# The opening of a gated-conv and pooling decoder step: loads held to two in flight per queue, transposes written ahead of matmuls, norms in pairs, and later weights in unused rows

## The chip, the cores and the metric

The kernel runs on the 8 cores of one Trainium2 chip. Each core takes one prompt sequence of 2048 tokens and 128 sampled tokens (16 short sequences of 8), and holds all weights in turn; the cores exchange nothing. The metric is the device time of the slowest core in microseconds. Below, TensorE is PE, VectorE is DVE, ScalarE is ACT, GpSimd is POOL and SyncE is SP.

## The reference

```python
def layer(x, ...):
    h = rmsnorm(x, g_pre_mix)
    p = h @ w_in                      # columns [xv | B | C | u | gate_conv | gate_pool], 1024 each
    z = C * xv
    y = B * (z[t-2]*w0 + z[t-1]*w1 + z[t]*w2)          # causal conv of width 3, per channel
    ya = y @ w_out_conv
    yb = pool_scale * groupwise_linear(trailing_mean(u) - u)   # windows 2, 4, 8, 16
    merged = sigmoid(gate_conv) * ya + sigmoid(gate_pool) * yb
    x = x + rmsnorm(merged @ w_o, g_post_mix)
    f = jnp.square(jax.nn.relu(rmsnorm(x, g_pre_mlp) @ w_up)) @ w_down     # 1024 -> 4096 -> 1024
    return x + rmsnorm(f, g_post_mlp)
```

The model width is 1024, the inner MLP width 4096, the depth 1. The last rows of z and u go out as new state.

## The kernel before

A core's 2176 tokens are 17 **tiles** of 128 tokens, x tile 0 to 16. All work is recorded in program order by a small layer (`Prog`) that derives each wait from overlapping rows of SBUF or PSUM; every engine then runs its own instructions strictly in the order in which they were recorded. Since helpers record the operations, the lines of the profile are those of the helpers: L144 is a matmul, L148 a transpose on PE, L161 an activation, L164 a DVE operation on two tensors, L169 one on a tensor and a scalar, L174 one with a scalar and two tensors, L553 a reciprocal, L129 any DMA.

The conv part comes first. Its weights are 8 column blocks j; for each, three chunks c = 0, 1, 2 (the columns of xv, C and B), each 512 KB in HBM and 256 KB once cast to bf16. One unit (j, tg) is column block j over a group tg of 512 tokens: 3 x 8 matmuls into three PSUM banks, then `a_ew` on ACT and DVE: copy xv (ACT), z = C * xv (DVE), the first conv tap cv0 (ACT), then whatever is in the list `mid`, then the taps cv1 and cv2 and the product Ap with B (all three DVE).

An x tile i becomes usable to PE in these steps: load (SP), `x_stat` (square-sum and square root, both ACT), `x_scale` (reciprocal on DVE, then the normalised tile xn on DVE or, where the call says "act", on ACT), `x_tr` (8 transposes on PE into one bank, then evacT on DVE, which copies it to SBUF). `x_norm` is stat and scale together.

The opening (`head`, `head2`, `head3`) runs units (0, 0), (1, 0), (0, 1) and (2, 0) while the first 8 tiles are still arriving. There, `h_mm(j, tg, c, subs)` issues 8 matmuls of 128 columns for each tile in `subs`; with `None` in place of a list it issues 8 of 512 columns. 22 dummy matmuls (`warm`) run first. From the first 512-column matmul of unit (2, 0) on, all units follow one another at 24 matmuls of 512 columns each.

Loads: SP issues x tiles 0 to 7 without a wait. POOL issues the nine chunks of j = 0, 1, 2 without a wait, then chunk (3, 0), which waits for x tile 7; SP's tile 8 waits for chunk (3, 0). Chunks of j = 4 to 7 go where a planner (`Arena`) puts them. It places every later weight load in SBUF, in 220 trials with varied preferences, and issues each load at the step where its rows have come free; the best plan is the one with the lowest cost for loads that come later than a wanted lead. The loads of the conv chunks have no lead: for these it takes the place that is free earliest and, between equals, the lowest address. All weight loads but those of w_down's products are issued by POOL; these, the x tiles, and the reloads of the first residual (x1) are issued by SP.

The last part, w_down for the second half of the tokens, is a series of steps of 16 matmuls of 512 columns. The second last product's weights are (2, q) and the last one's (6, q), q = 0 to 3, of 512 KB each; the first step that uses the (6, q) needs all four, at its matmuls 1, 5, 9 and 13. Their rows come free late, from products 1 and 7 and from x1 tiles (8 to 11) that a DVE addition has used up.

Of the kernel before, what the change touches and what calls it, by code (L numbers as in the profile page):

```python
# [273 lines left out]
class Arena:  # L274
# [19 lines left out]
    @staticmethod  # L294
    def place(keys, first, last, needs, fixed, trial):
        blocks = [(a // UNIT, -(-(a + n) // UNIT), f, l) for a, n, f, l in fixed]
        off, at, cost, state = {}, {}, 0, trial * 7919 + 17
        top = AR_BYTES // UNIT
        for key in keys:
            need = needs[key]  # L300
            n, early = -(-need["n"] // UNIT), need.get("early", 0)
            f, l, lead = first[key], last[key] + need.get("hold", 0), need.get("lead")
            state = (state * 1103515245 + 12345) % (1 << 31)
            how = (state >> 16) % 4 if trial else 0
            best = None
            starts = sorted({0} | {b[1] for b in blocks} | {b[0] - n for b in blocks})
            for c in starts:
                if c < 0 or c + n > top:
                    continue
                free = early  # L310
                for lo, hi, bf, bl in blocks:
                    if lo < c + n and hi > c:
                        if bl < f:
                            free = max(free, bl + 1)
                        elif bf <= l:
                            free = None
                            break
                if free is None or free > f:
                    continue
                late = max(0, free - f + lead) if lead is not None else free  # L320
                cand = (late,) + ((-free, c), (c, 0), (-c, 0), (-free, -c))[how if lead is not None else 1]
                if best is None or cand < best[0]:
                    best = (cand, c, free)
            if best is None:
                return None
            _, c, free = best
            if lead is not None:
                cost += (100 * max(0, free - f + lead) // max(lead, 1)) ** 2 * need.get("cost", 1)
                free = max(free, f - lead)
            off[key] = c * UNIT  # L330
            at.setdefault(free, []).append((f, key))
            blocks.append((c, c + n, free, l))
        return cost, off, at


def build_program():
# [34 lines left out]
    def xsrc(i):  # L371
        return x_p[i * 128:(i + 1) * 128, :] if i < 16 else x_s[:, :]
# [5 lines left out]
    with stack:  # L378
# [49 lines left out]
        def bank():  # L428
            b = min((i for i in range(8) if i not in held), key=lambda i: bank_used[i])
            touch(b)  # L430
            return b
# [28 lines left out]
        def step(w, fn):  # L460
            steps.append({"w": w, "f": fn})
# [45 lines left out]
        xload = {}  # L507

        def load_x(i, deps=()):
            xload[i] = P.dma("sp", XS[i % 11], xsrc(i), "x%d" % (i % 11), name="xload", deps=deps)  # L510
# [22 lines left out]
        def to_hT(src, i, gcol):  # L533

            b = bank()
            pb = PS[:, b, :].bitcast(BF16)
            for k in range(KC):
                P.tr(pb[:, k * 128:(k + 1) * 128], src[:, k * 128:(k + 1) * 128], IDB[:, :], signal=(k == KC - 1))
            gb = bass.AP(CS, gcol, [[72, 128], [1, KC], [0, 128]])
            P.tt("dve", htile(i), pb.rearrange("p (k t) -> p k t", t=128), gb, ALU.mult,  # L540
                 name="evacT")
            touch(b)
# [3 lines left out]
        def x_stat(i):  # L546
            ss = x_ss[i] = stat()
            P.act(XN[i % 3], XS[i % 11], AF.Square, accum_out=ss, name="sq")
            P.act(ss, ss, AF.Sqrt, bias=cs(C_EPS), scale=1.0 / D, name="sqrt")

        def x_scale(i, eng="dve"):
            ss = x_ss[i]
            P.add("dve", lambda e: e.reciprocal(ss, ss), reads=[ss], writes=[ss], name="rstd")  # L553
            if eng == "act":
                P.act(XN[i % 3], XS[i % 11], AF.Identity, scale=ss, name="xn")
            else:
                P.ts(eng, XN[i % 3], XS[i % 11], ss, None, ALU.mult, name="xn")

        def x_norm(i, eng="dve"):
            x_stat(i)  # L560
            x_scale(i, eng)

        def x_tr(i):
            to_hT(XN[i % 3], i, C_GM)
# [10 lines left out]
        def a_keys(h, j):  # L575
            return [("a", h, j, c) for c in range(3)] if h == 0 else [("a", h, j)]

        def a_mm(j, tg, banks, cols=None, cset=(0, 1, 2)):
            h = 0 if tg < 2 else 1
            c0, n, kind = TGS[tg]  # L580
            lo, hi = cols or (0, n)
            for c in cset:
                wt = chunk(("a", 0, j, c), 0) if h == 0 else chunk(("a", h, j), c)
                for k in range(KC):
                    P.mm(PS[:, banks[c], lo:hi], wt[:, k, :], hx(k, c0 + lo, hi - lo), start=(k == 0), stop=(k == KC - 1))
# [58 lines left out]
        def h_mm(j, tg, c, subs):  # L644
            bk = hb.setdefault((j, tg), [])
            while len(bk) <= c:
                bk.append(bank())
                held.add(bk[-1])
            if subs is None:
                a_mm(j, tg, bk, None, (c,))  # L650
            else:
                for s_ in subs:
                    a_mm(j, tg, bk, (s_ * 128, s_ * 128 + 128), (c,))

        def h_ew(j, tg, mid=()):
            held.difference_update(hb[j, tg])
            a_ew(j, tg, hb.pop((j, tg)), mid)

        def head():
            for z in Z + [ZX]:  # L660
                P.memset("dve", z[:, 0:2], 0.0)
            warm(22)
            x_norm(0)
            x_norm(1)
            x_tr(0)
            h_mm(0, 0, 0, (0,))
            x_tr(1)
            h_mm(0, 0, 1, (0,))
            x_norm(2, "act")
            h_mm(0, 0, 0, (1,))  # L670
            h_mm(0, 0, 1, (1,))
            h_mm(0, 0, 2, (0, 1))
            x_tr(2)
            x_norm(3)
            for c in range(3):
                h_mm(0, 0, c, (2,))
            x_tr(3)
            h_mm(1, 0, 0, (0, 1, 2))
            x_norm(4, "act")
            for c in range(3):  # L680
                h_mm(0, 0, c, (3,))
            x_tr(4)
            h_mm(1, 0, 0, (3,))
            h_mm(1, 0, 1, (0, 1, 2, 3))
            x_norm(5)
            h_ew(0, 0, [lambda: x_tr(5)])
        step(a_keys(0, 0) + a_keys(0, 1), head)

        def head2():
            h_mm(1, 0, 2, (0, 1, 2, 3))  # L690
            x_norm(6, "act")
            h_ew(1, 0, [lambda: x_tr(6)])
            for s_ in range(2):
                for c in range(3):
                    h_mm(0, 1, c, (s_,))
            x_norm(7)
        step(a_keys(0, 0) + a_keys(0, 1), head2)

        def head3():
            for c in range(3):  # L700
                h_mm(0, 1, c, (2,))
            x_tr(7)
            h_mm(2, 0, 0, None)
            for c in range(3):
                h_mm(0, 1, c, (3,))
            h_ew(0, 1)
            h_mm(2, 0, 1, None)
            h_mm(2, 0, 2, None)
            h_ew(2, 0)
# [620 lines left out]
        wl = {}  # L1330
# [5 lines left out]
        def issue(key, deps=()):  # L1336
# [13 lines left out]
            dst = arv(off, BF16, list(src.shape[1:])) if len(src.shape) == 3 else arv(off, BF16, [n])  # L1350
            wl[key] = P.dma("pool", dst, src, "w%d" % off, name="wload", deps=deps)

        for i in range(8):
            load_x(i)
        for s, st in enumerate(steps):
            for _, key in W.at.get(s, ()):
                deps = ()
                if key == ("a", 0, 3, 0):
                    deps = [xload[7]]
                issue(key, deps)  # L1360
                if key == ("a", 0, 3, 2):
                    for i in range(8, 11):
                        load_x(i, [wl[("a", 0, 3, 0)]] if i == 8 else ())
                if key == ("a", 0, 7, 2):
                    P.dma("pool", WPG[:, :, :, :], w_pg, "wpg")
            for first, i0 in ((n_u0 + 17, 0), (n_u1 + 18, 12)):
                if first <= s < first + 4:
                    load_xl(i0 + s - first, "xa%d" % (s - first))
            st["f"]()
            if s in u_steps:  # L1370
                unit(u_steps[s])
# [56 lines left out]
```

How the kernel before makes its waits and increments, by code:

```python
    def emit(self, stack):  # L185
# [33 lines left out]
                            continue  # L219
                        key = d.eng
                        val = d.wait_val
                        assert val is not None, (d.name, op.name)
                    if waited.get(key, 0) >= val:
                        continue
                    if need.get(key, 0) < val:
                        need[key] = val
                for key, val in need.items():
                    waited[key] = val
                    eng.wait_ge(sems[key], val)
                    nwait += 1
                if op.fn is not None:
                    ins = op.fn(eng)
                    if op.dma is not None:
                        ins.then_inc(sems[("dma", op.dma[0])], 16)
                    elif op.signal:
                        ins.then_inc(sems[e], 1)
        return nwait
```

## Time and profile before

| What | us |
|---|---|
| median of 3 runs (960.63 to 1078.2) | 961.12 |
| the profiled execution, its own time | 960.17 |
| its span on the slowest core, core 5 | 959.1 |
| busy time of PE, core 5 | 938.4 |
| busy time of DVE, core 5 | 640.3 |
| busy time of ACT, core 5 | 354.2 |

The span runs from the first to the last instruction of one core; the time of an execution is that of the slowest core and 1.07 us more. The profile is one execution. The spans of the other seven cores in it are 954.3 to 958.4 us. The highest of the three runs lies in a disturbed state of the chip and is compared with nothing.

### The profile page before, as it was taken

How to read it: one execution, taken by the hardware profiler on the slowest of the kernel's cores; microseconds unless marked ns; L12 is line 12 of the kernel's file. 1: busy time of each engine (PE TensorE's matmuls, PEld its weight loads, DVE VectorE, ACT ScalarE, POOL GpSimd, SP SyncE). 2: the span in 40 equal slices, each digit the busy share in tenths (PEclk: the TensorE clock that was granted, in tenths of full speed). 3: DMA queues.
4: the chain of work that ended last, by engine and by line, in shares of the span. 5: the costliest groups of instructions: out<-in, count | busy, mean ns of one | idle time of the engine just before them, and what ended most of it. 6: DMA issues, size and time to landing. Idle time of an engine off the chain costs nothing.

```text
span 959.1 us, 15642 instructions; the slowest of 8 cores (954.3 to 959.1 us)
## 1 busy us (share of the span) xinstructions
PE 938.4 (98%) x5158; PEld 463.5 (48%) x5158; DVE 640.3 (67%) x1017; ACT 354.2 (37%) x707; POOL 51.4 (5%) x99
## 2 busy tenths in 40 slices
PE   6899999999999999999999999999999999999997
PEld 4744544444455455455544444444444545544443
DVE  2568886885677777678735655670778887662687
ACT  4344332222433444333334444422023656731032
POOL 2031000000000000000000000000000000000000
PEclk7799999999999999999999999999999999999999
DMA  9999689859889998755227775375692973363683
GB/s 226 256 186 196 132 178 178 165 132 155 152 180 201 192 201 184 119 147 122 78 44 165 169 182 112 86 247 153 163 259 86 165 134 102 102 198 101 188 286 150
DMA packets 70687, 155.13 MB, mean 162 GB/s; under 512 B 22480, under 2 KB 41168, under 8 KB 68304
## 3 DMA queue, kind: packets, MB, share of 16 engines
q0 software_dynamic: 13104, 57.15, 36.1%
q1 hardware_dynamic: 56064, 92.49, 32.7%
q10 hardware_dynamic: 1440, 4.49, 1.2%
q8 instruction: 43, 0.70, 0.3%
q14 instruction: 36, 0.29, 0.1%
HBM read 173.11 MB, written 33.69 MB: 216 GB/s over the span
## 4 chain that ended last, share of the span: by engine, by line
PE 91%; DVE 3%; DMA 2%; issue 2%; ACT 1%; POOL 0%; DVEq 0%; ACTq 0%; POOLq 0%; SPq 0%
PE PS L144 90%; DVE AR L164 2%; DMA AR<-w_a 2%; DVE AR L174 1%; PE PS L148 1%; DMA AR<-wd_d 1%; ACT AR L161 1%; POOL AR L129 0%; ACT WPG L161 0%; DVEq L229 0%; DVE STAT L1002 0%; DVE AR L169 0%; ACT STAT L161 0%; DVE STAT L553 0%; POOL AR L514 0%
## 5 line engine op out<-in xcount | busy, mean ns | idle before, releaser
L144 PE MATMUL PS<-AR 128*128 128x512 bf16 (+1 forms) x4920 | 915.7, 348 | 8.0 <-DMA AR<-w_a 5.1
L144 PEld LDWEIGHTS PS<-AR 128*128 128x128 bf16 x4920 | 444.8, 99 | 468.7 <-issue 12.8
L164 DVE TENSOR_TENSOR AR<-AR 128x512 bf16<-128x512 f32 (+13 forms) x353 | 263.7, 778 | 52.2 <-ACT AR L161 34.2
L164 DVE TENSOR_TENSOR AR<-PS,AR 128x512 f32<-128x512 f32 (+1 forms) x235 | 145.3, 642 | 128.8 <-PE PS L144 96.0
L161 ACT ACTIVATE AR<-PS 128x512 f32<-128x512 f32 (+2 forms) x217 | 126.7, 606 | 237.8 <-PE PS L144 205.7
L161 ACT ACTIVATE AR<-AR 128x1024 bf16<-128x1024 f32 (+4 forms) x123 | 93.5, 766 | 145.9 <-DVE AR L164 122.7
L161 ACT ACTIVATE AR<-PS,CS 128x512 f32<-128x512 f32 (+1 forms) x80 | 48.9, 621 | 76.8 <-PE PS L144 64.0
L174 DVE SCALAR_TENSOR_TENSOR AR<-AR,CS 128x512 f32<-128x512 f32 (+1 forms) x80 | 53.7, 671 | 29.8 <-ACT AR L161 13.2
L161 ACT ACTIVATE AR<-AR,CS 128x512 f32<-128x512 f32 (+1 forms) x40 | 26.3, 658 | 98.0 <-DVE AR L164 80.2
L174 DVE SCALAR_TENSOR_TENSOR AR<-AR,STAT 128x1024 bf16<-128x1024 f32 (+2 forms) x35 | 43.8, 1254 | 4.2 <-DVE STAT L451 1.4
L174 DVE SCALAR_TENSOR_TENSOR AR<-AR 128x512 bf16<-128x512 f32 (+4 forms) x52 | 30.5, 587 | 5.6
L451 DVE RECIPROCAL STAT<-STAT 128x1 f32<-128x1 f32 x34 | 5.4, 159 | 42.7 <-ACT STAT L161 42.7
L164 DVE TENSOR_TENSOR AR<-PS,CS 128x1024 bf16<-128x1024 bf16 x17 | 20.7, 1219 | 17.1 <-PE PS L148 17.0
L164 DVE TENSOR_TENSOR AR<-WPG 128x512 bf16<-128x512 f32 (+1 forms) x27 | 16.7, 629 | 20.2 <-ACT WPG L161 20.2
L129 POOL DMA_DIRECT2D AR<-w_up x16 | 8.4, 528 | 341.1 <-PE PS L144 206.2
L174 DVE SCALAR_TENSOR_TENSOR AR<-PS,CS,AR 128x512 f32<-128x512 f32 (+1 forms) x40 | 26.5, 662 | 0.0
L161 ACT ACTIVATE WPG<-PS 128x512 f32<-128x512 f32 x34 | 19.9, 586 | 15.0 <-PE PS L144 13.0
L129 POOL DMA_DIRECT2D AR<-w_a x32 | 17.1, 559 | 130.5 <-PE PS L144 99.6
L174 DVE SCALAR_TENSOR_TENSOR AR<-PS,STAT,AR 128x1024 f32<-128x1024 f32 x17 | 21.8, 1283 | 2.4 <-DVE STAT L451 1.6
L161 ACT ACTIVATE STAT<-STAT,CS 128x1 f32<-128x1 f32 x67 | 19.7, 294 | 6.0
L144 PE MATMUL PS<-AR,WPG 128*128 128x512 bf16 (+1 forms) x80 | 21.2, 347 | 0.0
L148 PE MATMUL PS<-IDB,AR 128*128 128x128 bf16 x136 | 12.0, 240 | 3.6 <-ACT AR L161 3.3
(45 smaller groups left out, 130.7 us busy)
## 6 DMA issues: line engine op xcount, KB each, us to landing
AR<-wd_d SPq DMA_DIRECT2D x56, 512.0 KB, 5.7
AR<-x_p SPq DMA_DIRECT2D x32, 512.0 KB, 7.9
AR<-w_up POOLq DMA_DIRECT2D x16, 1024.0 KB, 11.2
wd_d<-AR SPq DMA_DIRECT2D x16, 896.0 KB, 8.7
AR<-w_m POOLq DMA_DIRECT2D x16, 768.0 KB, 9.6
x_d<-AR SPq DMA_DIRECT2D x17, 512.0 KB, 4.3
AR<-x_d SPq DMA_DIRECT2D x17, 512.0 KB, 9.6
AR<-w_dn POOLq DMA_DIRECT2D x16, 512.0 KB, 10.3
```

Of the source, the lines that this page charges most:

```text
L129: op = self.add(q, lambda e: e.dma_start(out=out, in_=in_, **kw), reads=[in_], writes=[out], name=name, dma=(semkey, cnt))
L144: return self.add("pe", lambda e: e.matmul(out, lhsT, rhs, start=start, stop=stop, skip_group_check=skip), reads=[lhsT, rhs], writes=[out] ...
L148: return self.add("pe", lambda e: e.transpose(out, in_, ident), reads=[in_, ident], writes=[out], signal=signal, name="tr")
L161: return self.add("act", lambda e: e.activation(out, in_, func, **kw), reads=rd, writes=wr, name=name)
L164: return self.add(eng, lambda e: e.tensor_tensor(out, in0, in1, op), reads=[in0, in1], writes=[out], name=name)
L174: return self.add(eng, lambda e: e.scalar_tensor_tensor(out, in0, scalar, in1, op0, op1), reads=rd, writes=[out], name=name)
L451: P.add("dve", lambda e: e.reciprocal(ss, ss), reads=[ss], writes=[ss], name="rstd")
```

## The change

`head` and `head2` are written in another order: both transposes of tiles 0 and 1 stand before the first matmuls, matmuls go tile by tile and not chunk by chunk, the norms are called in pairs, and the norms of tiles 6 and 7 are in the `mid` lists of units (0, 0) and (1, 0), where transposes of tiles 5 and 6 stood. x tiles 2 to 7 wait for the tile two before, chunks 2 to 8 for the chunk two before. The planner now prefers, for loads without a lead and between places that are free equally early, rows that no earlier load has used.

```diff
@@ Arena.place @@
-                free = early
+                free = 0
...
-                if free is None or free > f:
+                if free is None or max(free, early) > f:
                     continue
+                used, free = free, max(free, early)
                 late = max(0, free - f + lead) if lead is not None else free
-                cand = (late,) + ((-free, c), (c, 0), (-c, 0), (-free, -c))[how if lead is not None else 1]
+                cand = (late,) + ((-free, c), (c, 0), (-c, 0), (-free, -c), (used, c))[how if lead is not None else 4]
@@ head, head2, head3 @@
             x_norm(0)
             x_norm(1)
             x_tr(0)
-            h_mm(0, 0, 0, (0,))
             x_tr(1)
-            h_mm(0, 0, 1, (0,))
-            x_norm(2, "act")
-            h_mm(0, 0, 0, (1,))
-            h_mm(0, 0, 1, (1,))
-            h_mm(0, 0, 2, (0, 1))
+            for s_ in range(2):
+                for c in range(3):
+                    h_mm(0, 0, c, (s_,))
+            x_norm(2)
+            x_norm(3)
             x_tr(2)
-            x_norm(3)
+            h_mm(1, 0, 0, (0, 1))
+            x_tr(3)
             for c in range(3):
                 h_mm(0, 0, c, (2,))
-            x_tr(3)
-            h_mm(1, 0, 0, (0, 1, 2))
-            x_norm(4, "act")
+            h_mm(1, 0, 0, (2,))
+            x_norm(4)
+            x_norm(5, "act")
             for c in range(3):
                 h_mm(0, 0, c, (3,))
             x_tr(4)
             h_mm(1, 0, 0, (3,))
             h_mm(1, 0, 1, (0, 1, 2, 3))
-            x_norm(5)
-            h_ew(0, 0, [lambda: x_tr(5)])
+            x_tr(5)
+            h_ew(0, 0, [lambda: x_norm(6)])
...
             h_mm(1, 0, 2, (0, 1, 2, 3))
-            x_norm(6, "act")
-            h_ew(1, 0, [lambda: x_tr(6)])
+            x_tr(6)
+            h_ew(1, 0, [lambda: x_norm(7)])
             for s_ in range(2):
                 for c in range(3):
                     h_mm(0, 1, c, (s_,))
-            x_norm(7)
+            x_tr(7)
...
             for c in range(3):
                 h_mm(0, 1, c, (2,))
-            x_tr(7)
             h_mm(2, 0, 0, None)
@@ the loads @@
+        chunks = []
         for i in range(8):
-            load_x(i)
+            load_x(i, [xload[i - 2]] if i > 1 else ())
...
-                if key == ("a", 0, 3, 0):
+                if key[:2] == ("a", 0) and key[2] < 3:
+                    chunks.append(key)
+                    if len(chunks) > 2:
+                        deps = [wl[chunks[-3]]]
+                elif key == ("a", 0, 3, 0):
                     deps = [xload[7]]
```

PE in the opening before, from the warm-up to the first 512-column matmuls (`PS<-IDB` is the warm-up, L148 the transposes of one tile):

```order
L144 MATMUL PS<-IDB 128x512 x22
L148 MATMUL PS<-IDB,AR 128x128 x8
L144 MATMUL PS<-AR 128x128 x8
L148 MATMUL PS<-IDB,AR 128x128 x8
L144 MATMUL PS<-AR 128x128 x40
L148 MATMUL PS<-IDB,AR 128x128 x8
L144 MATMUL PS<-AR 128x128 x24
L148 MATMUL PS<-IDB,AR 128x128 x8
L144 MATMUL PS<-AR 128x128 x48
L148 MATMUL PS<-IDB,AR 128x128 x8
L144 MATMUL PS<-AR 128x128 x40
L148 MATMUL PS<-IDB,AR 128x128 x8
```

The same stretch of PE now:

```order
L144 MATMUL PS<-IDB 128x512 x22
L148 MATMUL PS<-IDB,AR 128x128 x16
L144 MATMUL PS<-AR 128x128 x48
L148 MATMUL PS<-IDB,AR 128x128 x8
L144 MATMUL PS<-AR 128x128 x16
L148 MATMUL PS<-IDB,AR 128x128 x8
L144 MATMUL PS<-AR 128x128 x56
L148 MATMUL PS<-IDB,AR 128x128 x8
L144 MATMUL PS<-AR 128x128 x40
L148 MATMUL PS<-IDB,AR 128x128 x8
L144 MATMUL PS<-AR 128x128 x32
L148 MATMUL PS<-IDB,AR 128x128 x8
```

The last line of the first list is tile 5, and the last of the second tile 6. The 48 matmuls behind tiles 0 and 1 are one block whose third group of 8 reads chunk 2; before, 32 of them stood ahead of chunk 2's first use.

DVE from the norm of tile 5 to the second product Ap before (the line with `128x8x128` is an evacT, `PS,AR 128x512` is z or Ap, L174 is cv1 and cv2):

```order
L553 RECIPROCAL STAT<-STAT 128x1
L169 TENSOR_SCALAR AR<-AR,STAT 128x1024
L164 TENSOR_TENSOR AR<-PS,AR 128x512
L164 TENSOR_TENSOR AR<-PS,CS 128x8x128
L174 SCALAR_TENSOR_TENSOR AR<-AR,CS 128x512 x2
L164 TENSOR_TENSOR AR<-PS,AR 128x512
L553 RECIPROCAL STAT<-STAT 128x1
L164 TENSOR_TENSOR AR<-PS,AR 128x512
L164 TENSOR_TENSOR AR<-PS,CS 128x8x128
L174 SCALAR_TENSOR_TENSOR AR<-AR,CS 128x512 x2
L164 TENSOR_TENSOR AR<-PS,AR 128x512
```

DVE now, from the evacuations of tiles 4 and 5 to the same product:

```order
L164 TENSOR_TENSOR AR<-PS,CS 128x8x128 x2
L164 TENSOR_TENSOR AR<-PS,AR 128x512
L554 RECIPROCAL STAT<-STAT 128x1
L169 TENSOR_SCALAR AR<-AR,STAT 128x1024
L174 SCALAR_TENSOR_TENSOR AR<-AR,CS 128x512 x2
L164 TENSOR_TENSOR AR<-PS,AR 128x512
L164 TENSOR_TENSOR AR<-PS,CS 128x8x128
L164 TENSOR_TENSOR AR<-PS,AR 128x512
L554 RECIPROCAL STAT<-STAT 128x1
L169 TENSOR_SCALAR AR<-AR,STAT 128x1024
L174 SCALAR_TENSOR_TENSOR AR<-AR,CS 128x512 x2
L164 TENSOR_TENSOR AR<-PS,AR 128x512
```

The evacT of tile 5 stood behind z of unit (0, 0) and now stands before it; the reciprocal and xn of tile 6, and later of tile 7, now stand between z and cv1. The ACT instructions of these two norms likewise stand behind cv0 of their unit.

SP's last loads before (`wd_d` 128x2048 is one (p, q) weight load, `x_d` a reload of x1):

```order
L129 DMA AR<-x_d 128x1024 x3
L129 DMA AR<-wd_d 128x2048 x4
L129 DMA AR<-x_d 128x1024
L129 DMA AR<-wd_d 128x2048 x3
L129 DMA AR<-x_d 128x4x256
L129 DMA AR<-wd_d 128x2048
L129 DMA AR<-x_d 128x4x256
L129 DMA AR<-x_d 128x1024
```

SP's last loads now:

```order
L129 DMA AR<-x_d 128x1024 x3
L129 DMA AR<-wd_d 128x2048 x4
L129 DMA AR<-x_d 128x1024
L129 DMA AR<-wd_d 128x2048 x2
L129 DMA AR<-x_d 128x4x256
L129 DMA AR<-wd_d 128x2048
L129 DMA AR<-x_d 128x4x256
L129 DMA AR<-wd_d 128x2048
L129 DMA AR<-x_d 128x1024
```

The planner's new plan moves one load each: (6, 1) from behind (6, 0) to the place that (6, 2) had, which waits for the addition of tile 8; (6, 2) to the place of (6, 3), which waits for the addition of tile 9; and (6, 3) behind one more x1 load, where it waits for the last step of product 7 on PE.

## Rows read from the trace of the kernel before

**Rows 1.** Spans of two of the cores, us, and their mean granted clock

```profile
core 1: 958.4 us, clock 0.994
...
core 5: 959.1 us, clock 0.987
```

**Rows 2.** Timeline of PE, opening, core 5: start us, us, instruction, idle before

```profile
15.41 2.72 PE L144 MATMUL PS<-AR 128*128 128x128 bf16 x24 [1.18 <-DMA AR<-w_a]
...
18.97 1.87 PE L144 MATMUL PS<-AR 128*128 128x128 bf16 x16 [0.83 <-DMA AR<-w_a]
...
23.17 2.72 PE L144 MATMUL PS<-AR 128*128 128x128 bf16 x24 [1.48 <-DVE STAT L553]
...
32.68 0.61 PE L148 MATMUL PS<-IDB,AR 128*128 128x128 bf16 x8 [0.29 <-DVE AR L169]
33.13 1.95 PE L144 MATMUL PS<-AR 128*128 128x128 bf16 x32
38.38 1.01 PE L148 MATMUL PS<-IDB,AR 128*128 128x128 bf16 x8 [3.31 <-ACT AR L161]
39.19 6.53 PE L144 MATMUL PS<-AR 128*128 128x128 bf16 x72
...
46.00 1.24 PE L144 MATMUL PS<-AR 128*128 128x512 bf16 x5
```

**Rows 3.** Busy time by stretch, core 5; last columns: PE's granted clock, DMA share, GB/s

```profile
18.90:27.00 8.10, 6.55 (x61) 6.35 (x62) 2.20 (x4) 0.74 (x3) 0.65 (x2) 0.50 1.04 225
27.00:37.30 10.30, 7.79 (x134) 7.39 (x132) 7.18 (x11) 5.23 (x10) 0.95 (x2) 1.00 1.03 190
37.30:44.10 6.80, 5.71 (x55) 5.75 (x56) 4.82 (x7) 3.48 (x6) 0.00 (x0) 0.50 1.04 354
```

**Rows 4.** Timeline of PE, core 1: tile 7 transposed, and the wait near the end

```profile
43.16 0.61 PE L148 MATMUL PS<-IDB,AR 128*128 128x128 bf16 x8
...
929.84 4.48 PE L144 MATMUL PS<-AR 128*128 128x512 bf16 x20 [2.46 <-DMA AR<-wd_d]
```

**Rows 5.** Issues of single weight chunks: 2.0 to 2.3 us, then 48.9 to 49.2 us

```profile
AR<-w_a POOLq DMA_DIRECT2D x1, 256.0 KB, 10.7
...
AR<-w_a POOLq DMA_DIRECT2D x1, 256.0 KB, 4.8
```

**Rows 6.** Timeline of all engines, 31 to 37 us, core 5

```profile
31.41 0.15 DVE L553 RECIPROCAL STAT<-STAT 128x1 f32<-128x1 f32 x1
31.67 0.75 DVE L169 TENSOR_SCALAR AR<-AR,STAT 128x1024 bf16<-128x1024 f32 x1
32.34 0.68 DVE L164 TENSOR_TENSOR AR<-PS,AR 128x512 f32<-128x512 f32 x1
...
33.12 0.72 ACT L161 ACTIVATE AR<-AR,CS 128x512 f32<-128x512 f32 x1 [1.83 <-DVE AR L164]
...
33.40 1.22 DVE L164 TENSOR_TENSOR AR<-PS,CS 128x1024 bf16<-128x1024 bf16 x1 [0.37 <-PE PS L148]
33.75 1.04 ACT L161 ACTIVATE AR<-AR 128x1024 bf16<-128x1024 f32 x1
34.54 1.60 DVE L174 SCALAR_TENSOR_TENSOR AR<-AR,CS 128x512 f32<-128x512 f32 x2
...
34.98 0.30 ACT L161 ACTIVATE STAT<-STAT,CS 128x1 f32<-128x1 f32 x1
36.24 0.69 DVE L164 TENSOR_TENSOR AR<-PS,AR 128x512 bf16<-128x512 f32 x1
```

**Rows 7.** Issue of one weight load of product 6, 922.0 to 922.4 us, core 5

```profile
AR<-wd_d SPq DMA_DIRECT2D x1, 512.0 KB, 8.2
```

**Rows 8.** Timeline, 921 to 931 us, core 5: SP's queue and PE

```profile
922.03 0.33 SPq L129 DMA_DIRECT2D AR<-wd_d  x1
922.82 5.95 SPq L129 DMA_DIRECT2D AR<-x_d  x4
...
930.52 0.81 PE L144 MATMUL PS<-AR 128*128 128x512 bf16 x3 [0.77 <-DMA AR<-wd_d]
```

## The prediction

> **What bounds the kernel now.** I read the spans of the cores first, then PE's timeline through the opening, then the granted clock there, and last the places late in the run where PE waits for a load. PE is busy for 938.4 of core 5's 959.1 us [rows 1], so only the some 20 us in which it isn't, and the stretches in which it runs at half its clock, can be won or lost by a change that removes no work. I call three moments of the opening A, B and C. A is the first use of weight chunk 2, at 18.97 us, which the landing of that chunk set; B is the end of the transposes of tile 5, at 32.68 + 0.61 = 33.29; C is the first 512-column matmul, at 46.00 [rows 2]. Behind C PE has no wait of a microsecond until the last products, so a microsecond at C is one at the end. The reader should see in these rows three kinds of loss before C: waits for chunks (0.83 before A), waits in the ring PE, DVE, ACT (1.48 at 23.17, 3.31 at 38.38), and a low clock: 24 matmuls take 2.72 us at 23.17, and the granted clock is 0.50 (the 1.2 GHz level) from 18.9 to 27.0 and from 37.3 to 44.1, and 1.00 (2.4 GHz) between [rows 3]. At the high level 8 instructions take 33.13 - 32.68 = 0.45 us, 0.056 each; at the low one 2.72 / 24 = 0.113 [rows 2]. The slowest core, 5, is so by its clock and its C: core 1 reaches C at 43.16 + 0.45 = 43.6 and still has a span of 958.4, since it loses 2.46 near the end [rows 1, 4].
>
> **Two in flight.** Of x tiles and chunks, each waits for the second before it. DMA share is 1.04 and 1.03 from 18.9 to 37.3 [rows 3]: the 16 engines are the limit while both queues have work, and two loads in each keep them at work as long as the third is issued and reaches the engines before the second is done. A chunk issued into an empty queue lands after 4.8 us, the first of all after 10.7 [rows 5]. Chunk 2 will be issued when chunk 0 has landed, at about 2.0 + 10.7 = 12.7. Its landing is then between 12.7 + 4.8 = 17.5 and, if it is only drawn on when chunk 1 has landed (at 15.4 by PE's wait for it [rows 2]) and pays 4.8 from there, 20.2. I take A as before, 18.97, since the engines are as full as before; the ends are -1.4 and +1.3. Queued behind the waits are, on SP, only the other x tiles, and on POOL the later chunks and then the chunks of j = 3 to 7; chunk (3, 0) waits for tile 7 as before. Tiles 8 and up and the blocks from j = 3 on are needed behind C, by over 15 us, so I cost their lateness at nothing; that cover is gone only if tile 8 is 15 us late. The Trainium skill (DMA: Bandwidth & Descriptors, section "Anatomy of one DMA — SWDGE (gpsimd) path") speaks against such waits: each DMA issued by GpSimd has a fixed cost of about 2.0 us, which a wait for its completion brings into the open, plus its bytes over 436e3 per us. By it chunk 2 would land 2.0 + 0.6 = 2.6 us behind chunk 0, at 15.3, and the time be some 3.6 us lower than mine; the rows (4.8 in an empty queue) don't agree, and I go by them.
>
> **From A to B.** Before, A to B is 14.3 us. Now 176 instructions stand there in one run: 32 matmuls, tile 2, 16, tile 3, 56, tile 4, 40, tile 5. That is 16 matmuls more than before, since tile 1's matmuls on chunks 0 and 1 now stand behind chunk 2's wait; the idle 1.48 behind tile 2 is filled by 16 matmuls of unit (1, 0). At the high clock 176 take 9.9, at the low one 19.9. Before, on core 5, the clock rose at 27.0, 3.9 us after the unbroken stretch that began at 23.17 [rows 2, 3]; now such a stretch begins at A. So I take 3.9 us at the low level (34 instructions), 142 x 0.056 = 8.0 at the high one, and 0.6 for the wait of tile 2's matmuls on its evacT (1.22 [rows 6], less the 24 instructions ahead of it, and pauses of the issue): 12.5, B = 31.5. The ends are 29.0 and 39.
>
> **From B to C.** This is the term that grows. Before, z of unit (0, 0) stood ahead of tile 5's evacT on DVE, and the norm of tile 6 was done on ACT meanwhile; PE then waited 3.31 for xn of tile 6 and was late with 72 matmuls at the low clock [rows 2]. Now evacT of tile 5 comes ahead of z, and the squares of tile 6 stand behind cv0 on ACT, which waits for z; xn of tile 6 stands ahead of cv1 on DVE, and the same again for unit (1, 0) and tile 7. From the starts in [rows 6], behind B: 0.11 to evacT, 1.14 to z, 0.78 to cv0, 2.16 from cv0's start to the end of the root (33.12 to 35.28), 0.1 to the reciprocal, 0.26 to xn (31.41 to 31.67): 4.55. Then 0.67 to cv1 (as xn to z), 1.70 to Ap (34.54 to 36.24), 0.69 to evacT of tile 6, 1.14 to z of unit (1, 0): 8.75. Then again 0.78, 2.16, 0.1 and 0.26 to xn of tile 7: 12.05, and 0.75 and 0.25 until PE transposes tile 7: 13.05. PE's own work up to there, 32 + 48 matmuls and tile 6, is done before that even at the low clock. Behind it come 0.45 for the transposes and 24 matmuls of unit (0, 1) which before stood ahead of tile 7: 1.4 at the high clock, 2.7 at the low one. C = B + 14.9 to B + 16.2; PE is idle twice for over 1.5 us on the way, as it was before its low clock at 37.3, so I take 15.4: C = 46.9. On core 5 that is 0.9 later than 46.00; on core 1, which had no clock loss ahead of tile 6, 3.3 later than 43.6 [rows 4].
>
> **The planner.** The chunks of j = 4 to 7 go to unused rows, and POOL's issue of 12 chunks no longer waits for PE. PE waited for none of them, so that gains nothing. But the other loads are planned anew, and most of the last ones come a step later. Load (6, 3) was issued at 922.03, landed 8.2 us later [rows 7] and let PE wait 0.77 before the last 4 matmuls of its step [rows 8]. 20 matmuls of 512 columns take 4.48 there, 0.22 each [rows 4]. That step began at 930.52 - 0.77 - 12 x 0.22 = 927.1, and the step before, of 16, at 923.6. Now (6, 2) is issued at 922.03 instead and lands at 930.3; PE needs it 8 matmuls into the step, at 928.9, and waits 1.4. (6, 3) is issued only when PE has ended product 7, at 923.6, behind the x1 load at 922.82. With 8.2 again it lands at 931.8, and later if it queues; I take 933. PE comes to it at 930.3 + 0.9 = 931.2 and waits 1.8. The sum is 3.2 for 0.77: +2.4 on core 5. On core 1, where the same load cost 2.46 [rows 4], I take +3.0. The ends are 0 (a later issue that meets less traffic) and +6.
>
> **Sum.** Core 5: 959.1 + 0.9 + 2.4 = 962.4. Core 1: 958.4 + 3.3 + 3.0 = 964.7, now the slowest [rows 1]. An execution takes 1.07 more than its slowest span (960.17 for 959.1): 965.8. The profiled execution lay 0.95 under the median of the runs; I add little for that: **966**.
>
> **Rivals.** First, *the first chunks come sooner* (faster). With two x tiles queued in place of eight, chunk 0 may not need 10.7 us; at the 4.8 of an empty queue it lands at 6.8 and chunk 2 by 13, and x tiles set the pace: tile 5, which has kept its place, lets B come at about 27.5, C at 43, 4 us below my sum on every core: 962, and with the end unmoved 958. It decides once chunk 2 lands before 16. Against it: x tiles and chunks already shared engines that were full. The Trainium skill (the same page, section "Queues, rings and completion order") says that each DMA engine takes packets in turn from the queues that have work; by that rule the depth of a queue doesn't change the shares, which speaks against this rival too, though no row of mine separates queues. Second, *the parts cancel*: the clock rises by chunk 1's matmuls, or DVE's chain overlaps more than I think, and the loads at the end find less traffic: 961. Third, *the clock stays low*: PE idles from chunk to chunk ahead of A, and if the 1.2 GHz level held up to B, B would be at 38.9 and C at 54, 7 us over my sum: 973.
>
> **How the numbers follow.** My forecast (963 to 971) gets 0.57, the cancelling parts (959 to 963) 0.2, sooner chunks 0.13, the low clock 0.1. The range 958 to 971 leaves out the low clock and half of the sooner chunks, 0.16. Two per cent, about what a measurement of this kernel can tell from no change, are 19 us, from 942 to 980. No case reaches either; for what I haven't seen I leave 0.015 on each side.
>
> **What would show it.** In the changed profile A should stand within 1.5 of 19.0 with PE waiting for `w_a`; a stretch without gaps from A to B with the low clock only at its start; then PE idle ahead of the transposes of tiles 6 and 7, both ended by DVE's xn, and C near 47. Near 930 there should be one or two waits for `wd_d` with 2 to 6 us in all. I am wrong if C is before 44 on core 1, if chunk 2 lands before 16, or if PE doesn't wait for tile 7.

## The result, and the profile after

The changed kernel takes 968.74 us (median of 4 runs, 968.05 to 969.38) against 960.63 for the kernel before (959.62 to 961.12), measured beside it: a ratio of 1.0086, 95% interval 1.0066 to 1.0106. It is slower by some 8 us. As everywhere below, disturbed runs are left out of the medians and the ratio. The forecast was 966, with a range of 958 to 971.

The spans of three cores of the profiled execution, which answer to [rows 1]:

```profile
core 1: 964.0 us, clock 0.989
core 2: 967.0 us, clock 0.987
...
core 5: 966.1 us, clock 0.990
```

Core 1 ends 5.6 us later than before and core 5 7.0; core 2, which took 954.3 before, is now the slowest. To see where the time went I cut each core's span in two, at the end of tile 8's transposes (the first tile behind the opening). Means over the eight cores, from the timeline of PE on each:

| | before | changed | difference |
|---|---|---|---|
| transposes of tile 5 end (B) | 31.7 | 28.7 | -3.0 |
| transposes of tile 8 end | 71.2 | 72.4 | +1.2 |
| from there to the last matmul | 878.2 | 884.0 | +5.8 |
| PE's waits over 0.1 us between 900 and 945 us, sum | 0.6 | 5.1 | +4.5 |

So most of the loss lies near the end of the run, and the opening gains first and then gives back more.

PE in the opening, core 5, to be held against [rows 2] (start us, us, instruction, idle before it and what ended that):

```profile
16.91 3.04 PE L144 MATMUL PS<-AR 128*128 128x128 bf16 x32 [3.13 <-DMA AR<-w_a]
...
28.08 0.61 PE L148 MATMUL PS<-IDB,AR 128*128 128x128 bf16 x8
28.53 1.95 PE L144 MATMUL PS<-AR 128*128 128x128 bf16 x32
35.09 1.01 PE L148 MATMUL PS<-IDB,AR 128*128 128x128 bf16 x8 [4.62 <-DVE AR L169]
35.90 3.85 PE L144 MATMUL PS<-AR 128*128 128x128 bf16 x48
42.50 0.61 PE L148 MATMUL PS<-IDB,AR 128*128 128x128 bf16 x8 [2.75 <-DVE AR L169]
```

A, the use of chunk 2, is at 16.91 in place of 18.97. From there to tile 5 PE has no wait. Then it waits 4.62 us for xn of tile 6 and 2.75 for xn of tile 7, both times for DVE.

Issues of chunk 0 (at 2.0 us) and of chunk 2 (at 10.8 us), core 5, with the time to landing, against the 10.7 of [rows 5]:

```profile
AR<-w_a POOLq DMA_DIRECT2D x1, 256.0 KB, 8.3
...
AR<-w_a POOLq DMA_DIRECT2D x1, 256.0 KB, 5.9
```

Chunk 0 lands 2.4 us sooner. Chunk 2, issued when chunk 0 has landed, takes 5.9 us and is there at 16.8, some 2 us sooner than the chunk that was issued without a wait.

Whose packets the 16 engines move meanwhile, from 8 to 10 us on core 5, before and then in the changed kernel (q0 is POOL's queue, with the chunks, q1 SP's, with the x tiles; packets, MB, share of the engines' time):

```profile
q0 software_dynamic: 87, 0.18, 56.4%
q1 hardware_dynamic: 90, 0.31, 48.8%
```

```profile
q0 software_dynamic: 175, 0.33, 106.5%
q1 hardware_dynamic: 4, 0.00, 0.6%
```

The engines are as full as before, but with other packets. Before, both queues have work and move about as many packets each. Now x tile 2 is issued only at 6.88, when tile 0 has landed, and its packets move from 10 us on. Until then SP's queue is empty, and the chunks have the engines to themselves. It is the same on every core: in these 2 us the chunks move 138 to 175 packets and the x tiles 4 to 11, where before the chunks moved 62 to 87 and the x tiles 66 to 90.

The chain behind tile 5, core 5, ACT and then DVE, against [rows 6]:

```profile
30.77 0.72 ACT L161 ACTIVATE AR<-AR,CS 128x512 f32<-128x512 f32 x1 [4.44 <-DVE AR L164]
31.40 1.04 ACT L161 ACTIVATE AR<-AR 128x1024 bf16<-128x1024 f32 x1
...
32.93 0.29 ACT L161 ACTIVATE STAT<-STAT,CS 128x1 f32<-128x1 f32 x1 [0.40 <-ACT AR L161]
```

```profile
29.94 0.68 DVE L164 TENSOR_TENSOR AR<-PS,AR 128x512 f32<-128x512 f32 x1
33.33 0.16 DVE L554 RECIPROCAL STAT<-STAT 128x1 f32<-128x1 f32 x1 [2.71 <-ACT STAT L161]
34.08 0.87 DVE L169 TENSOR_SCALAR AR<-AR,STAT 128x1024 bf16<-128x1024 f32 x1 [0.59 <-DVE STAT L554]
34.87 1.59 DVE L174 SCALAR_TENSOR_TENSOR AR<-AR,CS 128x512 f32<-128x512 f32 x2
```

These rows are one chain: z (29.94), cv0 (30.77), the squares of tile 6 (31.40), the root (32.93), the reciprocal (33.33), xn (34.08), and only then cv1 (34.87). DVE is idle 2.71 us of it and ACT was idle 4.44 ahead of it.

Busy time by stretch, core 5, of the changed kernel (columns as in [rows 3]): ahead of B, and near the end.

```profile
17.50:20.90 3.40, 3.40 (x36) 3.40 (x34) 0.25 (x1) 0.60 (x1) 0.90 (x2) 0.50 0.98 302
20.90:34.60 13.70, 9.56 (x168) 9.25 (x165) 7.07 (x10) 6.37 (x13) 5.80 (x11) 1.00 0.93 182
```

```profile
928.90:939.10 10.20, 5.25 (x13) 1.62 (x14) 0.76 (x2) 0.64 (x1) 0.00 (x0) 0.50 0.86 294
```

The granted clock rises 4.0 us behind A. Near the end it falls to 0.50, with PE idle for 7.3 of the 9.2 us from 926.5 to 935.7. The 13 matmuls of that stretch take 0.40 us each, against the 0.22 of [rows 4]. Before, the clock was granted in full there (core 5):

```profile
925.00:945.00 20.00, 19.23 (x91) 8.56 (x89) 15.83 (x22) 4.47 (x10) 0.00 (x0) 1.00 0.75 250
```

SP's queue and PE near the end, core 5, against [rows 8], and the issues of the loads (6, 2) and (6, 3) at 919.6 and 921.1 us, against the 8.2 of [rows 7]:

```profile
919.64 0.32 SPq L129 DMA_DIRECT2D AR<-wd_d  x1
920.37 0.52 SPq L129 DMA_DIRECT2D AR<-x_d  x1
921.05 0.57 SPq L129 DMA_DIRECT2D AR<-wd_d  x1
921.74 2.95 SPq L129 DMA_DIRECT2D AR<-x_d  x3
```

```profile
929.35 1.86 PE L144 MATMUL PS<-AR 128*128 128x512 bf16 x4 [2.84 <-DMA AR<-wd_d]
935.71 9.60 PE L144 MATMUL PS<-AR 128*128 128x512 bf16 x36 [4.50 <-DMA AR<-wd_d]
```

```profile
AR<-wd_d SPq DMA_DIRECT2D x1, 512.0 KB, 9.5
...
AR<-wd_d SPq DMA_DIRECT2D x1, 512.0 KB, 14.4
```

The two loads that come a step later than before let PE wait 2.84 and 4.50 us, where there was one wait of 0.77. The second of them takes 14.4 us from issue to landing. It stands behind another load, among four x1 loads and the stores of the results; which of these makes it so long was not tried.

### The profile page after: what moved, and what is told of

It reads as the page before. It is cut to its first block, busy times and chain, and to the rows that moved or that the text cites. A ratio compares the mean times of both kernels' runs of the same rounds, so it can differ in the third digit from the quotient of the medians.

```text
span 967.0 us, 15551 instructions; the slowest of 8 cores (959.3 to 967.0 us)
## 1 busy us (share of the span) xinstructions
PE 935.0 (97%) x5066; PEld 463.3 (48%) x5158; DVE 641.8 (66%) x1019; ACT 351.7 (36%) x705; POOL 51.6 (5%) x99
## 4 chain that ended last, share of the span: by engine, by line
PE 90%; DVE 4%; DMA 3%; issue 2%; ACT 1%; DVEq 0%; SPq 0%; POOL 0%; ACTq 0%; POOLq 0%
PE PS L144 90%; DVE AR L164 2%; DMA AR<-w_a 1%; DMA AR<-wd_d 1%; DVE AR L174 1%; PE PS L148 1%; ACT AR L161 1%; DVE AR L169 0%; ACT STAT L161 0%; DVEq L229 0%; SPq L129 0%; DVE STAT L1002 0%; DVE STAT L554 0%; POOL AR L515 0%; ACTq L229 0%
## 5 line engine op out<-in xcount | busy, mean ns | idle before, releaser
L161 ACT ACTIVATE AR<-PS,CS 128x512 f32<-128x512 f32 (+1 forms) x80 | 48.9, 621 | 77.2 <-PE PS L144 67.7
L174 DVE SCALAR_TENSOR_TENSOR AR<-AR,CS 128x512 f32<-128x512 f32 (+1 forms) x80 | 53.7, 671 | 29.5 <-ACT AR L161 13.4
L174 DVE SCALAR_TENSOR_TENSOR AR<-AR,STAT 128x1024 bf16<-128x1024 f32 (+2 forms) x35 | 43.8, 1254 | 4.1 <-DVE STAT L452 1.0
L174 DVE SCALAR_TENSOR_TENSOR AR<-AR 128x512 bf16<-128x512 f32 (+4 forms) x52 | 30.5, 586 | 6.0 <-DVE AR L164 0.6
L164 DVE TENSOR_TENSOR AR<-WPG 128x512 bf16<-128x512 f32 (+1 forms) x27 | 16.8, 629 | 19.7 <-ACT WPG L161 19.6
L174 DVE SCALAR_TENSOR_TENSOR AR<-PS,CS,AR 128x512 f32<-128x512 f32 (+1 forms) x40 | 26.5, 662 | 0.0
L174 DVE SCALAR_TENSOR_TENSOR AR<-PS,STAT,AR 128x1024 f32<-128x1024 f32 x17 | 21.8, 1284 | 3.0 <-DVE STAT L452 2.5
L148 PE MATMUL PS<-IDB,AR 128*128 128x128 bf16 x136 | 11.3, 231 | 9.1 <-DVE AR L169 9.1
## 6 DMA issues: line engine op xcount, KB each, us to landing
AR<-w_m POOLq DMA_DIRECT2D x16, 768.0 KB, 10.2
```

Of the source, the lines that this page charges most:

```text
L148: return self.add("pe", lambda e: e.transpose(out, in_, ident), reads=[in_, ident], writes=[out], signal=signal, name="tr")
L161: return self.add("act", lambda e: e.activation(out, in_, func, **kw), reads=rd, writes=wr, name=name)
L164: return self.add(eng, lambda e: e.tensor_tensor(out, in0, in1, op), reads=[in0, in1], writes=[out], name=name)
L174: return self.add(eng, lambda e: e.scalar_tensor_tensor(out, in0, scalar, in1, op0, op1), reads=rd, writes=[out], name=name)
```

## The experiments

The theory after the result: three parts act apart. The planner's new plan costs 6 to 8 us near the end; the limit of two in flight gains in the opening; the new order loses there, between B and C. The rival theories: the late waits are a product of the new opening, which shifts the traffic; or the limit only delays loads, and the tiles 6 and 7 are late by it. All kernels compute the whole layer. The table has each run's median, its ratio to the kernel before measured beside it, and means over the cores from the traces: landing of chunks 0 and 2, end of the transposes of tiles 5 and 8, and from there to the last matmul. No run differs from the kernel before by 2%; faster or slower below means that the interval of the ratio leaves out 1. The means are from one profile each. Three kernels are written alike up to tile 8 (changed, old plan, last loads dear) and have it at 72.4, 73.5 and 73.3, so a difference of a microsecond in one column shows nothing by itself.

| run | median | ratio (interval) | chunk 0 | chunk 2 | tile 5 | tile 8 | rest |
|---|---|---|---|---|---|---|---|
| before | | | 12.4 | 18.9 | 31.7 | 71.2 | 878.2 |
| changed | 968.74 | 1.0086 (1.0066 to 1.0106) | 9.7 | 16.5 | 28.7 | 72.4 | 884.0 |
| changed, old plan | 960.89 | 1.0011 (1.0000 to 1.0021) | 9.7 | 16.4 | 29.4 | 73.5 | 877.8 |
| plan only | 967.79 | 1.0080 (1.0063 to 1.0098) | 12.7 | 19.2 | 32.3 | 72.0 | 885.3 |
| limit only | 957.00 | 0.9971 (0.9961 to 0.9981) | 9.9 | 16.6 | 28.6 | 68.2 | 878.2 |
| order only | 962.87 | 1.0031 (1.0019 to 1.0044) | 12.6 | 19.1 | 31.4 | 75.2 | 877.7 |
| limit on x alone | 960.34 | 1.0000 (0.9989 to 1.0010) | 9.7 | 15.8 | 31.7 | 71.0 | 879.1 |
| limit on chunks alone | 963.84 | 1.0040 (1.0024 to 1.0056) | 12.6 | 22.0 | 36.2 | 75.8 | 878.2 |
| three in flight | 959.42 | 0.9989 (0.9978 to 1.0000) | 11.9 | 18.7 | 31.4 | 70.9 | 878.2 |
| changed, last loads dear | 961.17 | 1.0013 (1.0003 to 1.0023) | 10.0 | 16.5 | 29.1 | 73.3 | 877.8 |
| old plan, norms ahead | 956.98 | 0.9967 (0.9951 to 0.9983) | 9.9 | 16.7 | 28.9 | 68.8 | 877.7 |
| both norms ahead | 956.6 | 0.9963 (0.9949 to 0.9977) | 9.8 | 16.5 | 28.7 | 68.4 | 877.8 |

**The changed kernel with the old plan.** The new preference is taken back.

```diff
-                cand = (late,) + (..., (used, c))[how if lead is not None else 4]
+                cand = (late,) + (..., (used, c))[how if lead is not None else 1]
```

> The changed kernel with the planner's preference as it was before. Theory 1 (the loss is the planner's: late weight loads of w_down come a step later): the stretch from the transposes of tile 8 to the last matmul returns from a mean of 884.0 us over the cores to 878.2, the opening stays as in the changed kernel (tile 8 transposed at a mean of 72.4), and the time is 961 to 962, about that of the kernel before. Theory 2 (the late waits come from the new opening, which shifts the traffic of x1 loads and stores against PE): the stretch stays near 884 and the time at 967 to 969.

960.89: theory 1. PE's waits between 900 and 945 us are back at a mean of 0.7 us. On core 5 PE runs through the place without a wait:

```profile
914.76 30.59 PE L144 MATMUL PS<-AR 128*128 128x512 bf16 x141
```

**The plan alone.** The function `place` of the changed kernel, everything else as before.

> The kernel before with the planner's new preference alone. Theory 1 (the planner): the stretch from the transposes of tile 8 to the last matmul grows from a mean of 878.2 us to 883 to 885, the opening stays (tile 8 transposed at 71.2), time 966 to 969. Theory 2 (the new opening is needed for the late waits): the stretch stays near 878, time 960 to 962.

967.79: the plan alone, on the old opening, makes nearly all of the loss. The two waits are there, core 5:

```profile
928.87 1.02 PE L144 MATMUL PS<-AR 128*128 128x512 bf16 x4 [1.58 <-DMA AR<-wd_d]
933.30 12.04 PE L144 MATMUL PS<-AR 128*128 128x512 bf16 x46 [3.40 <-DMA AR<-wd_d]
```

**Last loads dear.** The planner takes the plan whose own sum of lateness is lowest, and that sum counts a late load of the last products like any other. This run keeps the new preference and weights eight loads.

```diff
-                    loads[("dn", half, p, q)] = dict(n=4096, lead=10 if p == 4 else 7)
+                    loads[("dn", half, p, q)] = dict(n=4096, lead=10 if p == 4 else 7, cost=4 if half == 1 and p in (2, 6) else 1)
```

> The changed kernel, with the planner's cost of lateness times four for the weights of products 2 and 6 of the second half. Its plan issues the loads (2, q) and (6, q) at the same steps as the kernel before; the conv chunks stay in unused rows, and the other early loads stand as in the changed kernel. Theory 1 (the loss near the end is the late issue of these eight loads): from the transposes of tile 8 to the last matmul 877.5 to 879 us (884.0 in the changed kernel), time 960 to 962. Theory 2 (something else in the new plan costs, as the chunks that no longer wait, or other late loads): 882 or more, time 965 or more.

961.17, and 877.8 for the rest of the run: theory 1. The chunks in unused rows and POOL's issue without a wait are still in this kernel, and cost nothing that can be seen. SP's queue, core 4, has no weight load behind the one at 919.92, and PE runs on (on core 5 a wait of 1.41 is left; the mean is 0.5):

```profile
919.92 0.32 SPq L129 DMA_DIRECT2D AR<-wd_d  x1
920.36 3.91 SPq L129 DMA_DIRECT2D AR<-x_d  x4
```

```profile
914.82 30.38 PE L144 MATMUL PS<-AR 128*128 128x512 bf16 x138
```

So the late issue of the last weights is what costs, not the use of other rows.

**The limit alone, and the order alone.** Each is the kernel before with one part of the change, copied as it stands in the diff.

> The kernel before with at most two x tiles and two chunks in flight alone. Theory 1 (fewer x tiles share the engines with the first chunks): chunk 2 lands at 16 to 17 in place of 18.9, the transposes of tile 5 end 1.5 to 2.5 us sooner (31.7 before), and those of tile 8 by about 1 to 2 sooner than 71.2; time 959 to 960. Theory 2 (what the changed kernel gains ahead of tile 5 comes from its order, and the waits only delay loads): tile 5 stays at 31.5 to 33, time 961 to 963.

> The kernel before with the new order of head, head2 and head3 alone. Theory 1 (order and limit act apart: the order shortens A to B by some 2 us and lengthens B to C by some 3 to 4): chunk 2 lands at 18.9 as before, the transposes of tile 5 end at about 30.5 to 31, those of tile 8 at 73.5 to 75 (71.2 before), time 963 to 965. Theory 2 (the order costs nothing by itself and the limit makes tiles 6 and 7 late): tile 8 at 71 to 72, time 960 to 962.

Both go the way of theory 1, but not by its sizes: the limit brings 3.0 us at tile 8 where 1 to 2 were expected (and 957.0 for 959 to 960), and the order hardly helps ahead of tile 5. First PE's waits for chunk 2 and for tile 6 on core 5 with the order alone, then the waits behind the transposes of tile 2 and ahead of those of tile 6 with the limit alone, which are as long as before (1.48 and 3.31):

```profile
19.30 3.26 PE L144 MATMUL PS<-AR 128*128 128x128 bf16 x32 [2.19 <-DMA AR<-w_a]
...
37.06 1.01 PE L148 MATMUL PS<-IDB,AR 128*128 128x128 bf16 x8 [4.37 <-DVE AR L169]
```

```profile
20.71 1.50 PE L144 MATMUL PS<-AR 128*128 128x128 bf16 x24 [1.48 <-DVE STAT L553]
...
34.73 1.01 PE L148 MATMUL PS<-IDB,AR 128*128 128x128 bf16 x8 [3.31 <-ACT AR L161]
```

The limit alone makes the kernel faster than before, 0.9971: chunk 2 lands 2.3 us sooner, tile 8 comes 3.0 us sooner (71.2 to 68.2), and the rest of the run stays at 878.2. The order alone makes it 4.0 us later (75.2). It hardly shortens the way from chunk 2 to tile 5 (31.4 - 19.1 = 12.3, before 31.7 - 18.9 = 12.8) and lengthens that from tile 5 to tile 8 from 39.5 to 43.8. I expected A to B to gain 2 us by the order. B is sooner in the changed kernel by the limit, through the landing of chunk 2.

**Which limit pays.** One queue limited at a time.

```diff
@@ limit on x alone: chunks as before @@
-            load_x(i)
+            load_x(i, [xload[i - 2]] if i > 1 else ())
@@ limit on chunks alone: x tiles as before @@
+        chunks = []
...
-                if key == ("a", 0, 3, 0):
+                if key[:2] == ("a", 0) and key[2] < 3:
+                    chunks.append(key)
+                    if len(chunks) > 2:
+                        deps = [wl[chunks[-3]]]
+                elif key == ("a", 0, 3, 0):
                     deps = [xload[7]]
```

> The kernel before with the limit on x tiles alone; the nine chunks are issued without a wait. Theory 1 (x tiles 2 and 3 no longer go ahead of the first chunks on the shared engines; the limit on chunks is no help): chunk 0 lands at 9 to 11 as with both limits, chunk 2 at 14 to 15 (16.6 with both limits), tile 8 is transposed at 67 to 69, time 955 to 957. Theory 2 (each queue has its share of the engines whatever its depth): chunk 0 lands at 12.4 and chunk 2 at 18.9 as before, tile 8 at 71 or later, time 960 to 962. Theory 3 (a deep queue of chunks takes the engines from x tiles 4 to 7): chunk 2 early, but tiles 6 and 7 late, tile 8 at 70 or later, time 959 or more.

> The kernel before with the limit on chunks alone; the eight x tiles are issued without a wait. Theory 1 (the limit on x tiles is what pays): chunk 0 lands at 12 to 13 as before, chunk 2 at 19 to 20.5, since it is issued when chunk 0 has landed and then takes some 6 us; tile 8 at 71 to 73, time 960 to 963. Theory 2 (the limit on chunks is what pays, by leaving the engines to the x tiles): tile 8 at 68 to 69.5, time 957 to 958.5.

I had expected the limit on x to pay alone. It brings the chunks sooner, as theory 1 of that run says (chunk 2 at 15.8), but theory 3 decides the time: nine chunks in their queue now make the x tiles late, and tile 5 is where it was before. From 11 to 16 us on core 5 the queues move 211 and 209 packets, and x tile 5 lands at a mean of 27.7 us (before 21.0, with both limits 22.1). The limit on chunks alone is worse than either theory had: chunk 2 at 22.0 and tile 8 at 75.8. On core 5 PE waits for tile 4 with the limit on x alone, and for chunk 2 with that on chunks alone:

```profile
27.61 0.61 PE L148 MATMUL PS<-IDB,AR 128*128 128x128 bf16 x8 [2.74 <-ACT AR L161]
```

```profile
22.70 1.87 PE L144 MATMUL PS<-AR 128*128 128x128 bf16 x16 [3.43 <-DMA AR<-w_a]
```

With the chunks alone limited, chunk 2 (issued at 13.15, when x tiles 0 to 2 have landed) takes 9.4 us beside the five x tiles still on their way:

```profile
AR<-w_a POOLq DMA_DIRECT2D x1, 256.0 KB, 9.4
```

Either limit alone gives 0 or a loss of 4.5 us at tile 8; both together give 3.0. What pays is that neither queue runs ahead of the other.

**Three in flight.** The diff is against the kernel with the limit alone.

```diff
-            load_x(i, [xload[i - 2]] if i > 1 else ())
+            load_x(i, [xload[i - 3]] if i > 2 else ())
...
-                    if len(chunks) > 2:
-                        deps = [wl[chunks[-3]]]
+                    if len(chunks) > 3:
+                        deps = [wl[chunks[-4]]]
```

> The kernel before with at most three x tiles and three chunks in flight in place of two (order and planner as before). Theory 1 (what pays is that neither queue runs ahead of the other): near the run with two, chunk 2 at 15.5 to 17, tile 8 at 68 to 69, time 956.5 to 958. Theory 2 (a third x tile already goes ahead of chunk 0 and takes its time on the engines): chunk 0 lands at 11 to 12.5, chunk 2 at 17 to 18.5, tile 8 at 69.5 to 71, time 958.5 to 960.5.

Theory 2: chunk 0 lands at 11.9, nearly as late as without a limit, and of the 3.0 us at tile 8 0.3 are left. The third x tile, issued at 2.0 us, keeps SP's queue at work beside chunk 0: from 8 to 10 us on core 5 it moves 67 packets to the chunks' 84, where with two in flight there were 4 to 175.

**Norms ahead.** The changed kernel with the old plan, and:

```diff
-            h_ew(0, 0, [lambda: x_norm(6)])
+            x_norm(6)
+            h_ew(0, 0)
...
-            h_ew(1, 0, [lambda: x_norm(7)])
+            x_norm(7)
+            h_ew(1, 0)
```

> The changed kernel with the planner's preference as it was before and with the norms of tiles 6 and 7 written ahead of the elementwise work of units (0, 0) and (1, 0) in place of inside it. Theory 1 (PE's waits of 4.4 and 1.5 to 2.5 us ahead of the transposes of tiles 6 and 7 come from the chain z, cv0, squares, root, reciprocal, xn): the first of them falls below 1.5, B to the transposes of tile 8 shrinks from 44 us by 3 to 5, tile 8 at 68.5 to 70.5, time 956 to 958. Theory 2 (tiles 6 and 7 are late because their loads are limited): the waits stay, tile 8 at 72 to 74, time 960 to 962.

956.98, tile 8 at 68.8 in place of 73.5, with the loads as limited as before: theory 1. PE ahead of tiles 6 and 7, core 5:

```profile
31.81 0.61 PE L148 MATMUL PS<-IDB,AR 128*128 128x128 bf16 x8 [0.69 <-DVE AR L169]
...
37.94 1.01 PE L148 MATMUL PS<-IDB,AR 128*128 128x128 bf16 x8 [2.84 <-DVE AR L169]
```

The wait for tile 6 has gone from 4.62 (4.50 with the old plan) to 0.69. That for tile 7 stays.

**Both norms ahead.** In addition the squares of tile 7 stand ahead of unit (0, 0), and its reciprocal and xn inside:

```diff
             x_norm(6)
-            h_ew(0, 0)
+            x_stat(7)
+            h_ew(0, 0, [lambda: x_scale(7)])
...
-            x_norm(7)
             h_ew(1, 0)
```

> The kernel of the run before with both norms ahead, with the squares and the root of tile 7 also ahead of unit (0, 0)'s elementwise work and its reciprocal and xn inside it, where DVE waits 0.99 us for cv0. Theory 1 (DVE's chain decides B to C to the end): PE's wait of 2.84 us ahead of tile 7 goes, tile 8 is transposed at 66 to 67.5 (68.75 with tile 6's norm alone out of the chain), time 954 to 956. Theory 2 (the squares of tile 7 hold up xv of unit (0, 0) on ACT, since tile 7 lands as late as 28 to 31 us, and the banks of unit (0, 1) come later by as much): PE waits for a bank in place of tile 7, tile 8 at 68.5 to 70, time 957 to 958.

Between the two: tile 7 is transposed 1.6 us sooner (36.7 in place of 38.3, means of the cores), but tile 8 only 0.4. On core 6 PE no longer waits for xn but for DVE's product Ap of unit (0, 0), which frees a bank:

```profile
36.49 0.61 PE L148 MATMUL PS<-IDB,AR 128*128 128x128 bf16 x8 [1.44 <-DVE AR L164]
```

That is theory 2's wait, though smaller than it said. The time of 956.6 can't be told from that of the run before it or of the limit alone; each of the three is faster than both kernels, than the kernel before by 0.3 to 0.4%. The limit and the old order together with the norms ahead was not tried, nor a better place for the last loads on top.

## Why the prediction came out right, step by step

The time (968.74 for 966) and the sign are those of the forecast. Its terms were less good: two were off, in opposite directions.

- **Chunk 2 at 18.97.** This step failed: "I take A as before, 18.97, since the engines are as full as before". A is at 16.91 on core 5, beyond the end of -1.4 that I gave and the 1.5 that I named as a sign. The landing of chunk 0 at 12.7 was held fast, and it moved: with two x tiles in flight it lands 2.4 us sooner. The rival of the sooner chunks had the mechanism, at a smaller size: it asked for chunk 2 before 16, and it is 16.5 in the mean (15.8 and 15.9 on cores 0 and 6). My argument against it was that the engines are full anyway. They are, but SP's queue runs empty between two x tiles, and the chunks get its share (175 packets to 4 from 8 to 10 us, before 87 to 90). The runs with the limit on x alone (chunk 0 at 9.7) and with three in flight (11.9) show the same: how long the other queue has work decides when the first chunk lands. The Trainium skill's rule (DMA: Bandwidth & Descriptors, section "Queues, rings and completion order") that each engine takes packets in turn from the queues with work was weighed in the same place. The traces agree with it while both queues have work, with 87 packets to 90. What failed is my step from it, that "the depth of a queue doesn't change the shares": a queue held to two in flight is without work part of the time.
- **The price of a chunk.** 4.8 us from issue to landing in an empty queue was the bound, 5.9 is measured. The Trainium skill's sum (the same page, section "Anatomy of one DMA — SWDGE (gpsimd) path"), an estimate of 2.6 us by its figures for 256 KB, is less than half of it; the trace decides.
- **A to B, 12.5.** 28.69 - 16.91 = 11.8: right, with the low clock only at its start, as said (3.4 us of it).
- **B to C, 15.4.** From the end of tile 5 to that of tile 7 plus 1.35 us for 24 matmuls at the high clock: 43.1 + 1.35 - 28.7 = 15.8 on core 5. The chain z, cv0, squares, root, reciprocal, xn is the one that I summed from [rows 6], and the run with the norms ahead shows it to be the cause.
- **The opening as a whole.** I had +0.9 on core 5 and +3.3 on core 1. By the transposes of tile 8 it is -1.7 and +1.5, mainly for the sooner chunk 2.
- **The last loads, +2.4 to +3.0.** This is the term that was mis-sized. Its mechanism is shown by three runs; its measure is +5.8 in the mean, +3.9 on core 1 and 887.03 - 878.46 = +8.57 on core 5, beyond my end of +6. Two things were missing. I gave (6, 3) the 8.2 us of the load before and 1 us for the queue; it takes 14.4. And I priced only the waits. On core 5 these are 7.34 - 0.77 = 6.57 of the 8.57. The clock fell to 0.50 at 928.9, 2.4 us into the first wait, and stayed there through the second until 939.1; the 13 matmuls in that stretch, at 0.40 us for 0.22, make up the other 2 us. In the mean of the cores 4.5 of the 5.8 us are waits, and the clock falls there on the other seven cores too (a mean of 0.83 to 0.91 from 925 to 945 us).
- **The unused rows at nothing.** Right: with the last loads priced higher they leave no mark.
- **The low clock up to B** did not happen; **the parts cancel** is what the opening alone does on some cores, but not the sum.

That the number came out so near was luck in part. The opening came out lower and the end higher than I had them, and the errors took each other away. And the sum was made for the wrong core: I had core 1 as the slowest, with 964.7 (it takes 964.0), and core 5 at 962.4 (966.1). The slowest in the profile is core 2 with 967.0, for which I made no sum; it loses 4.7 us up to tile 8 and 7.9 behind it.

## What to carry to other kernels

Where two queues feed the same DMA engines, look at the landing of the first transfer that PE waits for, and at how long the other queue has packets to move beside it: limiting both queues brought 3 us where limiting either brought none or a loss. When a planner's preference is changed for loads that don't matter, compare the whole new plan, above all the last loads of the program, which nothing behind them hides; here the new plan alone was 7 us slower, and weighting the loads whose wait ends last mended it. A norm placed inside another unit's elementwise chain joins two chains into one: price each hop from issue to issue, and put it ahead where its input is there already.

## What the runs showed of the hardware that was not expected

- The DMA engines move about as many packets of one queue as of the other while both have work (87 and 90 from 8 to 10 us, core 5, before), and a queue whose depth is limited leaves its share to the other while it is empty (175 and 4 in the changed kernel). So the depth of one queue sets the landing in the other: the first chunk, issued at 2.0 us, takes a mean of 10.4 us with eight x tiles issued without a wait, 9.9 with three in flight and 7.7 to 7.9 with two (changed, limit alone, limit on x alone). Later chunks on core 5 took 4.8 us with POOL's queue empty, 5.9 beside two x tiles and 9.4 beside five.
- Late in the run, on core 5 of the changed kernel, the granted clock fell from 1.00 to 0.50 within a wait of 2.84 us and stayed there for 10.2 us, through a second wait of 4.50. Before, with a wait of 0.77 at this place on core 5, and even with one of 2.46 on core 1, it stayed at 1.00. So such a wait can cost more than its own length.
